# Folding the final normalisation of a hybrid MoE encoder step into its expert chunks

## What is computed

```python
x = x + concat(out_a, out_b) @ w_out          # the mixers: some 850 us of the kernel, not touched
h2 = rms_norm(x, norm2_g)
# every token goes to 2 of 32 experts: 4352 (token, expert) pairs
y = sum over the token's two experts of gate * ((silu(h2 @ wg[e]) * (h2 @ wu[e])) @ wd[e])
x = x + y
return rms_norm(x, final_norm_g)              # mean of squares over 1024 columns, rsqrt, times the gain
```

## Time and profile before

| what | value |
|---|---|
| median of 3 runs | 1784.66 us (1784.59 to 1786.18) |
| profiled execution, from first to last instruction | 1787.2 us; the page gives no other time for it |
| mean granted TensorE clock | 0.969 |
| busy: PE, DVE, ACT, POOL | 1678.6, 603.5, 365.8, 348.5 us |
| moved by DMA | 322.25 MB, 180 GB/s over the span |

### The profile page before, as it was taken

How to read it: one execution, slowest core, us unless ns; L and a number is a source line. 1 busy time by engine, 2 the same in 40 slices (tenths; PEclk the granted TensorE clock), 3 DMA queues, 4 the chain that set the end, 5 groups by cost and what they waited for, 6 DMA issues and landing times.

```text
span 1787.2 us, 28410 instructions
## 1 busy us (share of the span) xinstructions
PE 1678.6 (94%) x10624; PEld 1434.2 (80%) x10624; DVE 603.5 (34%) x1770; ACT 365.8 (20%) x768; POOL 348.5 (19%) x535
## 2 busy tenths in 40 slices
PE   6999999999999999997599999999999999999960
PEld 4768676767676676765499999999999999999950
DVE  3536363545464554644311111111111111111114
ACT  2313131413132131322011111111111111111113
POOL 1101111111111010101112222222222222222235
PEclk9999999999999999998699999999999999999985
DMA  9410202011010101026288899999999999999968
GB/s 298 184 71 1 83 12 82 12 59 35 35 59 35 59 12 71 1 60 172 59 243 247 266 271 279 278 276 292 301 300 297 322 314 312 322 323 322 314 185 349
DMA packets 221004, 322.25 MB, mean 180 GB/s; under 512 B 24889, under 2 KB 173274, under 8 KB 220970
## 3 DMA queue, kind: packets, MB, share of 16 engines
q1 hardware_dynamic: 200538, 264.07, 44.6%
q0 software_dynamic: 17984, 48.81, 12.9%
q10 hardware_dynamic: 2448, 8.91, 1.2%
HBM read 268.97 MB, written 52.78 MB: 180 GB/s over the span
## 4 chain that ended last, share of the span: by engine, by line
PE 92%; DMA 2%; DVE 2%; POOL 1%; issue 1%; ACT 1%; SPq 0%; ACTq 0%; POOLq 0%; DVEq 0%
PE ps L834 28%; PE ps L696 18%; PE ps L847 14%; PE ps L757 13%; PE ps L719 7%; PE ps L856 3%; PE ps L818 2%; PE ps L779 2%; PE ps L729 2%; PE ps L683 1%; PE ps L771 1%; DMA w_in_sb<-acc_rows 1%; PE ps L742 1%; DMA out_y<-w_in_sb 0%; DMA acc_rows<-w_in_sb,idx_out 0%
## 5 line engine op out<-in xcount | busy, mean ns | idle before, releaser
L834 PE MATMUL ps<-w_out_sb,w_in_sb 128*128 128x128 f32 (+4 forms) x4096 | 510.2, 285 | 1.2 <-ACT w_out_sb L973 1.2
L834 PEld LDWEIGHTS ps<-w_out_sb,w_in_sb 128*128 128x128 f32 x4096 | 506.6, 190 | 1.5 <-issue 1.5
L696 PE MATMUL ps<-hT,w_in_sb 128*128 128x256 f32 (+1 forms) x1728 | 360.5, 369 | 3.2 <-issue 3.2
L696 PEld LDWEIGHTS ps<-hT,w_in_sb 128*128 128x128 f32 x1728 | 313.6, 191 | 46.4 <-issue 7.4
L847 PE MATMUL ps<-w_out_sb,w_in_sb 128*128 128x128 f32 (+4 forms) x2048 | 259.0, 287 | 0.0
L847 PEld LDWEIGHTS ps<-w_out_sb,w_in_sb 128*128 128x128 f32 x2048 | 252.5, 190 | 0.3
L757 PE MATMUL ps<-w_out_sb,catT 128*128 128x512 f32 x544 | 237.9, 598 | 4.8 <-DVE catT L1167 4.8
L334 POOL TENSOR_TENSOR pad<-mhalf 128x1 f32<-128x1 f32 x149 | 36.4, 245 | 1041.3 <-ACT h2T L882 240.3
L757 PEld LDWEIGHTS ps<-w_out_sb,catT 128*128 128x128 f32 x544 | 103.7, 192 | 132.6 <-issue 127.5
L1320 DVE TENSOR_TENSOR w_out_sb<-ps,w_out_sb 128x128 f32<-128x128 f32 (+4 forms) x128 | 39.4, 307 | 471.6 <-ACT w_out_sb L979 471.6
L1324 DVE COPY w_out_sb<-ps 128x256 f32<-128x256 f32 (+4 forms) x128 | 58.4, 456 | 224.0 <-PE ps L847 224.0
(11 more groups left out here) (184 smaller groups left out, 1266.4 us busy)
## 6 DMA issues: line engine op xcount, KB each, us to landing
w_in_sb<-in_w_gate SPq DMA_DIRECT2D x64, 1024.0 KB, 6.5
w_in_sb<-in_w_up SPq DMA_DIRECT2D x64, 1024.0 KB, 9.6
w_in_sb<-in_w_down SPq DMA_DIRECT2D x32, 1536.0 KB, 9.7
w_in_sb<-in_w_down SPq DMA_DIRECT2D x32, 512.0 KB, 10.4
xa<-in_x SPq DMA_DIRECT2D x17, 512.0 KB, 3.9
xr<-in_x SPq DMA_DIRECT2D x17, 512.0 KB, 3.4
acc_rows<-xr SPq DMA_DIRECT2D x17, 512.0 KB, 2.6
w_in_sb<-acc_rows SPq DMA_DIRECT2D x17, 512.0 KB, 8.2
```

The source lines that it names most:

```text
L696: mm = pe.matmul(bank[:, cc * n:(cc + 1) * n], w_in_v[:, k, col:col + P], hT[:, k, 0:n], start=(k == 0), stop=(k == KD - 1))
L834: mm = pe.matmul(bank[:, m * CH:m * CH + size], w[:, k, f * P:(f + 1) * P], xTm[:, k, :, 0:size // 2], start=(k == 0), stop=(k == KD - 1))
```

## The change

An expert chunk now reads its tokens' rows of `acc` into `part` (buffer of `xa`), adds, stores the sum to `acc` with a plain indirect DMA, and normalises the sum and writes it to `y` itself. A token has two experts: the chunk that comes first writes an unfinished row to `y`, the later one overwrites it with the full one. All indirect DMAs have a bounds check that skips empty slots, the rows of zeros are gone, and so is the last pass. DVE evicts all four banks `r{i}{h}`; ACT squares the sums instead. The final gain is loaded into `g1b` before the chunks.

POOL, in the place of what stood in its chunk loop (`carried(n)` waits for the carry before and does one):

```diff
             with pool.Fori(0, chunks) as q:
-                load_index(q, idx_out, io_loaded)
+                pool.wait_ge(nx_loaded, 16 * q + 16)
+                carried(5 * q + 1)
+                nc.gpsimd.tensor_copy(idx_out[:], idx_nx[:]).then_inc(io_ready, 1)
+                pool.wait_ge(io_ready, q + 1)
+                carried(5 * q + 2)
+                for h in range(2):
+                    pool.indirect_dma_start(part[:, h, :], None, acc,
+                                            bass.IndirectOffsetOnAxis(ap=idx_out[:, h, 0:1], axis=0),
+                                            bounds_check=NTOK - 1, oob_is_err=False).then_inc(part_loaded, 16)
+                load_index(q + 1, idx_nx, nx_loaded)
                 pool.wait_ge(xg_loaded, 32 * q + 64)
                 load_index(q + 2, idx_in, ix_loaded)
                 pool.wait_ge(ix_loaded, 16 * q + 48)
                 wait_full(pool, "chunk", q, "xT3")
...
                 gather()
-                wait_out(pool, "chunk", q, "r10")
-                wait_out(pool, "chunk", q, "r11")
...
+                for i in range(2):
+                    for h in range(2):
+                        wait_out(pool, "chunk", q, f"r{i}{h}")
+                carried(5 * q + 4)
                 for h in range(2):
                     pool.indirect_dma_start(acc, bass.IndirectOffsetOnAxis(ap=idx_out[:, h, 0:1], axis=0),
-                                            ysb[:, h, :], None, compute_op=ALU.add).then_inc(y_added, 16)
-                pool.wait_ge(y_added, 32 * q + 32)
+                                            ysb[:, h, :], None,
+                                            bounds_check=NTOK - 1, oob_is_err=False).then_inc(part_stored, 16)
+                pool.wait_ge(y_stored, 32 * q + 32)
+                pool.wait_ge(ysq_ready, 2 * q + 3)
+                carried(5 * q + 5)
+                nc.gpsimd.tensor_copy(idx_y[:], idx_out[:]).then_inc(iy_ready, 1)
+                nc.gpsimd.tensor_scalar(rstd[0:HF, 0:2], ssq[0:HF, 0:2], 1.0 / D, EPS, ALU.mult,
+                                        ALU.add).then_inc(yms_ready, 1)
+                pool.wait_ge(yms_ready, q + 1)
+                nc.gpsimd.tensor_tensor(rstd[0:HF, 0:2], rstd[0:HF, 0:2], mhalf[0:HF, 0:2], ALU.pow).then_inc(yrs_ready, 1)
+                pool.wait_ge(iy_ready, q + 1)
+                pool.wait_ge(yfin_ready, 2 * q + 2)
+                carried(5 * q + 6)
+                for h in range(2):
+                    pool.indirect_dma_start(a["y"], bass.IndirectOffsetOnAxis(ap=idx_y[:, h, 0:1], axis=0),
+                                            yfin[:, h, :], None,
+                                            bounds_check=NTOK - 1, oob_is_err=False).then_inc(y_stored, 16)
+                pool.wait_ge(part_stored, 32 * q + 32)
```

ACT and DVE at the end of a chunk:

```diff
-                act.wait_ge(io_loaded, 16 * q + 16)
-                for i in range(2):
-                    bank = wait_full(act, "chunk", q, f"r{i}0")
-                    nc.scalar.activation(ysb[0:size // 2, 0, i * BANK:(i + 1) * BANK], bank[0:size // 2, :], ACT.Copy,
...
+                for h in range(2):
+                    for i in range(2):
+                        wait_out(act, "chunk", q, f"r{i}{h}")
+                    act.wait_ge(ysq_ready, 2 * q + 1 + h)
+                    act.wait_ge(yrs_ready, q + 1)
+                    nc.scalar.activation(junk[0:size // 2, h], ysb[0:size // 2, h], ACT.Square,
+                                         accum_out=ssq[0:size // 2, h:h + 1]).then_inc(ysq_ready, 1)
...
-                dve.wait_ge(io_loaded, 16 * q + 16)
+                dve.wait_ge(io_ready, q + 1)
+                dve.wait_ge(part_loaded, 32 * q + 32)
                 for i in range(2):
-                    bank = wait_full(dve, "chunk", q, f"r{i}1")
-                    V.tensor_scalar(ysb[0:size // 2, 1, i * BANK:(i + 1) * BANK], bank[0:size // 2, :],
...
+                    for h in range(2):
+                        bank = wait_full(dve, "chunk", q, f"r{i}{h}")
+                        V.scalar_tensor_tensor(out=ysb[0:size // 2, h, i * BANK:(i + 1) * BANK], in0=bank[0:size // 2, :],
+                                                     scalar=idx_out[0:size // 2, h, 1:2].bitcast(F32),
+                                                     in1=part[0:size // 2, h, i * BANK:(i + 1) * BANK], op0=ALU.mult, op1=ALU.add)\
+                            .then_inc(read("chunk", f"r{i}{h}"), 1)
+                dve.wait_ge(yrs_ready, q + 2)
+                dve.wait_ge(y_stored, 32 * q + 32)
+                for h in range(2):
+                    V.scalar_tensor_tensor(out=yfin[0:size // 2, h], in0=ysb[0:size // 2, h], scalar=rstd[0:size // 2, h:h + 1],
+                                           in1=g1b[0:size // 2], op0=ALU.mult, op1=ALU.mult).then_inc(yfin_ready, 1)
```

SP, ahead of its chunk loop and behind it; POOL's, ACT's and DVE's `final` loops go with SP's:

```diff
-            sp.wait_ge(const_dve, 3)
-            for dst in (acc, h2_rows):
-                for h in range(2):
-                    r = NTOK + HF * h
-                    sp.dma_start(dst[r:r + HF], zrow[0:HF]).then_inc(table_ready, 16)
...
+            sp.wait_ge(xn_ready, GT * NPG + 1)
+            sp.dma_start(g1b[:], a["final_g"].broadcast_to([P, D])).then_inc(fg_loaded, 16)
             wait_out(sp, "plan", 0, "plan")
...
-            sp.wait_ge(moe_done, 1)
...
-            for b in range(FB):
-                load_f(0, b)
```

More of the change, by code:

```diff
@@ L44 @@
 N_PAD = 96
-FB = 8
+RG = 4
 class PsumJobs:
@@ L211, in hymba_step @@
         idx_out = sb("idx_out", [HF, 2, 2], U32)
+        idx_nx = sb("idx_nx", [HF, 2, 2], U32)
+        idx_y = sb("idx_y", [HF, 2, 2], U32)
         o = 0
@@ L231, in hymba_step @@
         tinit = aT[:].rearrange("p a b -> p (a b)")[:, 0:2 * CH].bitcast(U32).rearrange("p (n t) -> p n t", t=2)
-        zrow = qT[:].rearrange("p a b -> p (a b)")
-        fb = [w_in[:, b * D:(b + 1) * D] for b in range(FB)]
-        fsq = [w_in[:, (FB + b) * D:(FB + b + 1) * D] for b in range(FB)]
+        part = xa[0:HF]
+        yfin = xr[0:HF]
+        junk = ri[:].rearrange("p a b c -> p (a b c)")[0:HF].rearrange("p (h d) -> p h d", h=2)
         ps = [ctx.enter_context(nc.psum_tensor(f"ps{b}", [P, BANK], F32)) for b in range(BANKS)]
@@ L493, in _ @@
                     weights(e, piece)
-            sp.wait_ge(xn_ready, GT * NPG + 1)
-            sp.dma_start(g1b[:], a["final_g"].broadcast_to([P, D])).then_inc(fg_loaded, 16)
-            sp.wait_ge(moe_done, 1)
-            def load_f(it, b):
-                wait(sp, f_stored[b], 16 * it)
-                sp.dma_start(fb[b], acc[0:NTOK].rearrange("(n p) d -> n p d", p=P)[bass.ds(it * FB + b, 1)]
-                             .rearrange("a p d -> p (a d)")).then_inc(f_loaded[b], 16)
-            for b in range(FB):
-                load_f(0, b)
-            with sp.Fori(1, NTILE // FB) as it:
-                for b in range(FB):
-                    load_f(it, b)
-            load_f(NTILE // FB, 0)
             sp.wait_ge(state_out, 16 * (NC + 4))
@@ L515, in _ @@
                 sp.wait_ge(h2_stored[t], 16 * n)
-            for b in range(FB):
-                sp.wait_ge(f_stored[b], 16 * (NTILE // FB + (b == 0)))
         @block.gpsimd
@@ L667, in _ @@
-            with pool.Fori(0, NTILE // FB) as it:
-                for b in range(FB):
-                    final(it, b)
-            final(NTILE // FB, 0)
+                                            ysb[:, h, :], None,
[4 more added lines that the diff above has]
+                nc.gpsimd.tensor_copy(idx_y[:], idx_out[:]).then_inc(iy_ready, 1)
@@ L1334, in _ @@
                     chunk(q, size)
-            dve.wait_ge(fg_loaded, 16)
-            def final(it, b):
-                dve.wait_ge(f_rs, it * FB + b + 1)
-                V.scalar_tensor_tensor(out=fb[b], in0=fb[b], scalar=rstd[:, b:b + 1], in1=g1b[:],
-                                       op0=ALU.mult, op1=ALU.mult).then_inc(f_ready, 1)
-            with dve.Fori(0, NTILE // FB) as it:
-                for b in range(FB):
-                    final(it, b)
-            final(NTILE // FB, 0)
 def kernel(**inputs):
```

96 lines of the change are left out of this document (36 added, 60 removed).

## The result

The changed kernel takes 1791.21 us (median of 7 runs, 1787.02 to 1796.78) against 1784.64 us before (7 runs): ratio **1.0035**, 95% interval 1.0023 to 1.0047. It is slower by a third of a per cent where 1745 us, 2.2% faster, was predicted. The profiled execution, the slowest of the seven (1796.78), has a span of 1795.2 us against 1787.2 before.

The account below looks back on a forecast made before the run. PE was taken to bound the chunk loop, with an uncovered 62.40 us last pass behind it. Removing that pass gave -44.4 and POOL's longer round +5, so -39.4 from 1784.66: 1745 us, range 1736 to 1771.

Parts of the forecast that it names:

- DMA: Row transfers on POOL's queue in chunks of 128 slots: 5.0 to 9.3 us against 6.6, taken as no change.
- 6.8 us of early landing: Second weight piece in late chunks: lands at 1627.8, wanted at 1634.6, so the weights have 6.8 us spare.
- The tail: Behind PE's last transposes: the end comes 18.0 us after PE's instead of 62.4.
- this end: The kernel's close after the last `y` store lands: the forecast gave no time to anything behind that landing.
- -44.4: Gain in us from dropping the last pass, net of work behind the last chunk; bounds 40.9 to 46.4.
- POOL's round: POOL's steps per chunk of 128 slots: grow by 2.3 to 24.9 us against PE's 24.31, costing 5 us in all.
- DVE and ACT beside PE: Inside each chunk: DVE grows from 4.4 to about 8.5 us, ACT trades evictions for squares, both beside PE's 24.31.
- Chunks of 140 and 132 slots at PE's pace: Chunk loop: the longer POOL work fits these chunks, with spares of 5.5 and 3.5 us, so no loss.
- DMA becomes the bound: Rival, chance 0.15: at a 323 GB/s ceiling, 8.47 MB per chunk of 128 slots take 26.2 us; 20.1 lost, 1760 us.
- the sign that was named for it: PE idle ahead of line 834, waiting for weights, would show that DMA is the bound.
- Scatters cost what adds cost: Rival, chance 0.13: a plain store takes 1.53 us of POOL, not 0.98, adding 4.4 per chunk; 1771 us.
- Slower: POOL's round: Rival, chance 0.07: the bounds check makes all eight indirect DMAs per chunk take 1.5 instead of 1.0 us; 1811 us.

Follow-up runs that it names:

- one loop per size: Changed kernel with one POOL loop per chunk size, so a row DMA has half the chunk's slots as places, not 90: 1768.69 us, ratio 0.992.
- after, 2 KB rows: Changed kernel with only the weights altered, to come in 2 KB rows instead of 1 KB: 1772.40 us, ratio 0.9931.
- empty slots moved: Changed kernel with 180 more rows and no index out of bounds, so each row transfer moves all 180 rows: 1805.57 us in one run.
- rounded: Changed kernel with POOL loops by chunk size and row places rounded up to a multiple of 16: 1767.02 us, ratio 0.9889.
- rounded, 2 KB rows: Changed kernel with POOL loops by chunk size, places rounded up to 16, and weights in 2 KB rows: 1750.67 us, ratio 0.9818.
- no rows to `y`: Changed kernel with all indices of the stores to `y` past the end, so none of its rows is written: 1770.67 us.
- the same, 16 places: Changed kernel with no row of `y` written and 16 places instead of 90 in each of those empty stores: 1766.55 us.
- one loop per size, 2 KB rows: Changed kernel with POOL loops by chunk size and weights in 2 KB rows, nothing rounded: 1761.47 us, ratio 0.987.
- before, skipping: Kernel before the change, with a bounds check so that its gathers and adds skip empty slots: 1786.86 us.
- before, 2 KB rows: Kernel before the change, with weights in 2 KB rows: 1785.2 us.
- the quiet groups: Changed kernel plus groups of six 8 KB-row gathers behind the last chunk, nothing else moving: first 64 of 90 places took 23.5 us, 64 of 64 18.6.

## Why the prediction was wrong

The step that failed is the one on **DMA**. Its range for the rows was 5.0 to 9.3 us a chunk and it chose "no change" against 6.6. As a mean over 16 engines that is right: in the chunks of 128 slots the rows take 23.3% of 251 us, 6.5 us a chunk. The step failed in taking the mean, and in calling 6.8 us of early landing a spare: the up weights now land in a median of 18.0 us instead of 9.7, 8.3 later. The DMA view of these chunks, after, and with one loop per size:

```profile
q1 hardware_dynamic: 44207, 53.86, 69.4%
q0 software_dynamic: 8919, 17.85, 23.3%
...
w_in_sb<-in_w_up SPq DMA_DIRECT2D x16, 1024.0 KB, 18.0
```

```profile
q1 hardware_dynamic: 43976, 53.63, 75.0%
q0 software_dynamic: 6787, 17.58, 26.0%
```

Weights (q1) and rows (q0) of all versions, as shares of 16 engines' time in their chunks of 128 slots, and what the chain that ended last goes over there. (The share is the time of all packet records over 16 engines' time; records overlap, so it can exceed 100.)

| version | period, us | weights | rows | sum | chain over | with rows on 12 of 16 engines |
|---|---|---|---|---|---|---|
| after | 27.9 | 69.4 | 23.3 | 92.7 | weights | 100.5 |
| after, 2 KB rows | 26.2 | 68.0 | 23.7 | 91.7 | weights | 99.6 |
| empty slots moved | 28.6 | 67.4 | 33.9 | 101.3 | weights | |
| one loop per size | 25.7 | 75.0 | 26.0 | 101.0 | weights | |
| rounded | 26.7 | 74.8 | 25.2 | 100.0 | weights | |
| rounded, 2 KB rows | 24.6 | 72.9 | 26.3 | 99.2 | PE, weights | |
| no rows to `y` | 26.6 | 73.0 | 20.7 | 93.7 | POOL's round | 100.6 |
| the same, 16 places | 26.5 | 73.3 | 20.0 | 93.3 | POOL's round, PE | 100.0 |
| one loop per size, 2 KB rows | 25.2 | 70.7 | 26.1 | 96.8 | POOL's round, PE | |
| before | 24.3 | 75.1 | 27.1 | 102.2 | PE | |
| before, skipping | 24.3 | 74.3 | 19.1 | 93.4 | PE | 99.8 |
| before, 2 KB rows | 24.3 | 68.8 | 28.0 | 96.8 | PE | |

Only the versions whose chain goes over the weights say what the engines can give. Of these, the two with 64 valid of 90 places stop at 92 to 93%, the others at 99 to 101. The last column is the sum with the rows counted as if 12 engines had them (rows times 16/12; 12 is the usual number in flight for 64 of 90): then all of them stand at about 100%. So in the late chunks of the change the fullest engines are always busy: they have 8.7 us of rows a chunk where they had 6.6, and SP's queue waits for them while the others idle. That the same engines are the fullest during the chunks isn't shown directly, since a packet's record doesn't name its engine; it is worked out from the quiet groups and this table. Nor does a full share alone hold PE up: the kernel before runs at PE's pace with 102, and with skipping at 99.8 by the last column.

Uneven engines are only part of it. With one loop per size the rows take 0.260 x 25.7 = 6.7 us a chunk, as forecast, and fill the engines alike, and the weights still come too late for PE's pace: there had been no room on engines with a share of 102. It takes the 2 KB rows as well to come down to 24.6.

Point by point:

- *The tail*: 22.8 us against 18.0 forecast. The second `y` store starts 11.1 us after PE's end (11.8 forecast), so the chain of DVE, ACT and POOL was priced well. Its data move until 1787.1, 3.6 us after its start, sooner than the 6.2 taken. But the span ends 8 us after that, and what fills them is POOL's closing DRAIN, which the page doesn't count as busy; before and after (its duration in ns as min/median/max, then its start in us):

```profile
L118 POOLq DRAIN  x1: 7302/7302/7302, 1779.7 to 1779.7; - x1
L117 POOLq DRAIN  x1: 7263/7263/7263, 1787.7 to 1787.7; - x1
```

  Before, POOL issued its last root at 1779.7, and 4.2 us of its drain ran while the last rows were still being stored (their data end at 1783.9). After, it can start only when the last `y` rows have landed, so all 7.3 us of it come behind them. The forecast had put this end at nothing; -44.4 became -39.7.
- *POOL's round*: a round of 24.9 us and a loss of 5 us were forecast. The instructions cost what was said, but the round was mis-sized. The forecast had `part` land level with the first eviction; where the chain goes over the round (no rows to `y`) DVE waits for `part`, and the period is 26.6 us. In the change the weights are later still, so the round doesn't decide. With places rounded and 2 KB rows it holds nobody up: the nine chunks lose 221.6 - 218.8 = 2.8 us, of which 1.8 are waits for weights.
- *DVE and ACT beside PE*: right. DVE's 8 us a chunk hold nobody up.
- *Chunks of 140 and 132 slots at PE's pace*: wrong, by 3.6 and 13.1 us; PE waits for the same weights there (70 and 66 of 90 places are valid). With one loop per size those of 140 are back at 25.8, those of 132 are not.
- *The rivals*: "DMA becomes the bound" had the place, and the sign that was named for it, PE idle ahead of line 834, is what the trace shows. But its price took 323 GB/s as a ceiling on bytes, and gave 1760. Bytes don't set it: the rate fell to 286 GB/s where it should have held. "Scatters cost what adds cost" and "Slower: POOL's round" fall by the 0.95 to 1.07 us of the issues, "empty slots still move" by the version that does move them and is 14 us slower. Yet the last was half right: for the fullest engines a chunk of 128 slots holds as many rows as one of 180.

The forecast of 1745 was thus that of a kernel whose DMAs leave room. Row DMAs that fill all engines alike aren't enough for that (1768.69); with places rounded and wider weight rows as well it runs at 1750.67. That this comes near 1745 is in part luck, since the tail and POOL's round were mis-sized too.

## What to carry to other kernels

When PE keeps pace with DMA engines that are 100% busy, a landing that is early is no reserve: ask what each engine is given per round, not what all are given together. Don't give an indirect DMA many more places than it has valid ones: skipped places at the end leave their engines idle and the others as loaded as before. Of the numbers tried here 64 and 80 did well, 66 badly and 48 no better than 64. Where DMA is the bound, the width of the rows of the *largest* stream (here the weights) is worth as much as anything done to the small one. And after each remedy ask again what the chain goes over: behind the weights stood a round of landings on POOL that was only 1.3 us shorter. Last, what an engine does after its last instruction of the program is part of the span: a drain that was covered can come bare.

## What the runs showed of the hardware that was not expected

- Larger packets move more per second: in late chunks of the kernel before, 1 KB packets of weights beside rows made 323 GB/s; its last pass, with 4 KB packets, moved 420 GB/s in 1755:1775. Median packet times of the weights in 1530:1690 were 46 to 48 ns for 1 KB and 84 to 87 ns for 2 KB.
- Six gathers of 8 KB rows took 19.4 us for 48 places, 18.6 for 64, 24.8 for 66, 20.1 for 80 and 23.6 for 90, all valid: the fewest places are not the fastest. Packets took 846, 622, 798, 544 and 567 ns on average. Why they are slow with 48 and 66 places is open.
- Six indirect DMAs that move nothing still take 9.6 us, 7.6 of them POOL's issue (five steps of 1.32 and 1.01).
- POOL's closing DRAIN took 7.3 us in the kernels before and after, and 7.26 in the versions of the change (5.63 in the two with groups of gathers behind the last chunk).
